# Two-layer mixer kernel: conditioning half moved, norm squares added on GpSimd, two scalars computed first

## The chip, the cores and the metric

One Trainium2 chip, and one of its cores. The number is the device time of one execution in microseconds (us); all arithmetic is fp32 or made of fp32 parts. TensorE is PE below, VectorE DVE, ScalarE ACT, GpSimd POOL and the engine that issues the weight transfers SP.

## The reference

Two blocks run one after the other. The first (`first_block`) works on 256 latent and 256 context tokens of width 1024 in two layers, and the change touches it alone, but for the norms, which the second block has too. Cut to what matters:

```python
def rms_norm(x, g, eps):
    return x * lax.rsqrt(jnp.mean(x * x, axis=-1, keepdims=True) + eps) * g

def mixer(h_lat, h_ctx, ...):
    lam = exp(sum(lv[0] * lv[1])) - exp(sum(lv[2] * lv[3])) + lam_init
    ...
    fa = fourier_mix(h_lat @ w_fa)
    db = diff_post(diff_attention_latent(qb, kb, vb, lam))      # softmax(s0) - lam * softmax(s1)
    nc = neighbourhood_attention_latent(...)
    g_a, g_b, g_c = split(sigmoid(h @ w_g + b_gate), 3)
    return (g_a * (fa @ w_a) + g_b * (db @ w_b) + g_c * (nc @ w_c)) @ w_out

for l in range(2):
    mod, mod_c = silu_c @ w_ada[l] + b_ada[l], silu_cc @ w_ada[l] + b_ada[l]
    sh1, sc1, gt1, sh2, sc2, gt2 = split(mod, 6)
    h = h + gt1 * mixer(modulate(rms_norm(h, g_mix[l]), sh1, sc1), ...)
    h = h + gt2 * conv_ffn(modulate(rms_norm(h, g_ffn[l]), sh2, sc2))
x = rms_norm(h, g_final)
```

The second block has stick-breaking attention, sparse attention and two more feed-forwards, with four norms of its own. `silu_c @ w_ada[l]` is the conditioning: one row of 1024 against 1024 x 6144 weights, for latent and context at once.

## The kernel before, in words

Activations lie feature-major in SBUF, 8 row-blocks of 128 features by T tokens: T is 512 in layer 0 and in the norm that ends it, 256 afterwards. Weights come from memory in slabs of 1 MB (SP, L951, a ring of three raw buffers). A slab is cut into pieces of 128 x 1024 numbers; there are four places for pieces. ACT copies a piece's high part (`split`, L1304), DVE takes the low part (L1585), and PE multiplies high by high, low by high and high by low (L1026 to L1028) for every 128 rows. The last piece of a slab frees the raw buffer.

The order of the work is written out by `Plan` as one list of steps, and the program of every engine walks that list. Nothing overtakes on an engine. `finish(gen)` writes out all steps of a generator; `weave(main, filler, n_main, n_fill)` writes units of attention and, after each, a share of filler steps; `mixed(a, b)` takes one step of each in turn. `later(n, f)` puts a step off by n ticks; attention units and filler steps tick. A `split` step is written whenever a place for a piece is free at the moment at which a gemm or the conditioning asks for its next piece (`ahead()`, called by `piece()`), and nowhere else.

**Conditioning** (`ada`): per four column blocks two slabs of two pieces each, PE with 8 matmuls of 4 x 256 high and 8 low per slab (L1057, L1058). The result's rows are copied by ACT (`ada_rows`, L1317) into a square buffer, turned on PE two ticks later (`ada_turn`, L1066), and added to the bias by DVE (L1602, L1604, L1609). Layer 1's 48 column blocks, 24 filler steps, run woven into the feed-forward (FFN) of layer 0.

**Neighbourhood attention** (`na1`, `na2`, `attend_pv`): 32 units (8 heads by 4 query blocks) in layer 0. Scores on PE (L1157), exp on ACT (L1460), then the probabilities are turned on PE (L1125), copied by ACT to a square buffer (`pT`, L1435), and multiplied with the values on PE (`pv`, L1142), one tick after the turn. Its filler is the second half of q and k and `merge(1, "w_b", ...)`: four quarters of two gate steps (sigmoid on ACT, L1358) and two product steps each. Differential attention is built the same way (scores L1118, exp L1429), and in layer 0 its filler already mixes conditioning steps of layer 0 with merge steps.

**Norm** (`NormPlan`): ACT squares each row-block (L1328), PE sums over the features with a matmul against ones (L1075, 8 of them into one bank; the trace shows each as two records), ACT takes the root (L1333), DVE the reciprocal (L1613) and the product (L1621), ACT scales, and the low parts are made by DVE (L1626) for even row-blocks and by POOL (L995) for odd ones. There are 11 norms. Two compute all squares at once (`mix0`, T=512, and one of T=256 between the second block's parts). Four hang on gemms of eight pieces deep, each square behind its row-block (`ffn0`, T=512, and three of T=256). Five hang on the last gemm of a feed-forward (one of T=512, `mix1`; four of T=256), whose last accumulation is two pieces deep and whose row-blocks therefore follow one another within a few us.

**lam**: after the split of `mix0` and of `mix1`, the product of 64 x 2 numbers on DVE (L1631), a sum on PE (L1081), exp on ACT and a subtraction on DVE.

Buffers: eight PSUM banks, four `tmps`, two square buffers (`sqs`), two gate buffers (`gts`). Each is given to the step that takes it next in turn, with a wait for its last reader.

Of the kernel before, what the change touches and what calls it, by code (L numbers as in the profile page):

```python
# [9 lines left out]
F32R = mybir.dt.float32r  # L10
# [4 lines left out]
NR = 3  # L15
# [130 lines left out]
class Plan:  # L146
# [276 lines left out]
    def layer(self, l, nrm):  # L423
# [7 lines left out]
        lb = self.banks.take()  # L431
        self.add("lam", (l,), b=lb)
        self.banks.give(lb, ("lam_exp", l))
# [113 lines left out]
        filler = itertools.chain(na_qk(1), merge(1, "w_b", 4, lambda k: ("db", l, k)))  # L547
        self.weave(self.run_units([(h, qt) for h in range(8) for qt in range(nq)], na1), filler, 8 * nq, 4 + 16)
# [3 lines left out]
        for k in range(8):  # L552
# [10 lines left out]
                   self.ada(1, 0, 48) if l == 0 else iter(()), 32, 24)  # L563
# [229 lines left out]
class NormPlan:  # L793
    def __init__(self, plan, name, T, at_once=None):
        self.plan, self.name, self.T, self.b, self.n, self.square = plan, name, T, None, 0, None
        if at_once:
            for k in range(8):
                self.add(k, at_once)

    def add(self, k, after):  # L800
        q = self.plan.sqs.take()
        self.plan.add("sq", (self.name,), n=k, t=q, x=(self.T, self.n == 0 and self.square is None, after))
        self.sum()
        self.square = (q, k)
# [153 lines left out]
def pool_program(pool, on, c, plan):  # L958
# [11 lines left out]
    for s in plan.steps:  # L970
# [14 lines left out]
        elif s.kind == "bias":  # L985
# [5 lines left out]
            load(("bias", l, h), BI[:, (h % 2) * 512:(h % 2) * 512 + 512], dram["nab"][l, h])  # L991
        elif s.kind == "nlow" and s.n % 2:
# [12 lines left out]
def tensor_program(pe, on, c, plan):  # L1005
# [5 lines left out]
    for s in plan.steps:  # L1011
# [56 lines left out]
        elif kind == "sqsum":  # L1068
            i, k = s.n
            if i == 0:  # L1070
                for f in s.b.was:
                    on.wait_ge(*at(*f))
            on.wait_ge(*at("side", "consts"))
            on.wait_ge(*at("sq", id[0], k))
            pe.matmul(c.bank(s.b)[:, 0:s.x], ones, c.sq(s.t)[:, 0:s.x], start=i == 0, stop=i == 7).then_inc(  # L1075
                up("acc", ("sqsum", id[0], i)), 1)
        elif kind == "lam":
            for f in s.b.was:
                on.wait_ge(*at(*f))
            on.wait_ge(*at("lam_pp", *id))  # L1080
            pe.matmul(c.bank(s.b)[:, 0:2], ones[0:64, :], c.m["ST"][0:64, 20:22], start=True, stop=True).then_inc(  # L1081
# [205 lines left out]
def scalar_program(act, on, c, plan, nc):  # L1287
# [6 lines left out]
    for s in plan.steps:  # L1294
# [23 lines left out]
        elif kind == "sq":  # L1318
            T, first, after = s.x
            if first:  # L1320
# [240 lines left out]
def vector_program(dve, on, c, plan):  # L1561
# [15 lines left out]
    for s in plan.steps:  # L1577
# [513 lines left out]
```

## Time and profile before

| | us |
|---|---|
| median of 3 runs | 3034.61 |
| lowest and highest | 3031.26, 3041.79 |
| the profiled execution's time | 3040.34 |
| its span in the profile | 3038.5 |
| PE busy, PE weight loads busy | 2787.8, 2422.3 |
| DVE, ACT, POOL busy | 1754.9, 1406.3, 57.2 |
| mean granted clock of PE | 0.949 |

A row of the timeline is the start in us, the duration in us, engine, line, operation, target and sources, size and count, and in brackets how long the engine had been idle and what released it. Matmuls of PE overlap: a duration holds the latency of one, and the distance of two starts is their pace. In the waits view a row is engine, tile and line of the waiter, the engine, tile and line that released it, then us in total, times and the longest.

### The profile page before, as it was taken

Reading aid. Unit: us, or ns where it says so; the run is one execution under the profiler, and the core shown is the slowest. Engines: PE = TensorE matmul, PEld = TensorE weight load, DVE = VectorE, ACT = ScalarE, POOL = GpSimd, SP = SyncE. Lnnn points to the kernel's source line nnn. Section 1 sums busy time; section 2 is a strip of 40 time slices with the busy share of each in tenths; the row PEclk is TensorE's granted clock in tenths of the full one; section 3 lists DMA queues with packets and bytes.
Section 4 is the critical chain, followed back from the end, with each engine's and each line's share of the span. In section 5 each row is a group of like instructions: output and inputs, shape, how many; then the busy total and the mean of one; then the engine's idle time right before and its main releaser. Section 6 shows DMA issues by size and latency. Waiting matters only on the chain.

```text
span 3038.5 us, 42732 instructions
## 1 busy us (share of the span) xinstructions
PE 2787.8 (92%) x17980; PEld 2422.3 (80%) x17980; DVE 1754.9 (58%) x2928; ACT 1406.3 (46%) x2258; POOL 57.2 (2%) x75
## 2 busy tenths in 40 slices
PE   4997899998999997989989979989998999789999
PEld 2875576676777775877789979987998999667999
DVE  5255634345666665454568756656566657565565
ACT  5245635433444444464655544445444545433443
POOL 1000000000000000000000000000000000000000
PEclk7998999999999998999999989999999999776999
DMA  6223422121444432223345545542455555200454
GB/s 224 66 90 111 145 76 67 53 95 64 153 139 136 142 132 97 91 98 104 112 141 192 167 144 183 175 130 83 154 183 164 169 194 167 86 28 1 153 181 139
DMA packets 337391, 382.16 MB, mean 126 GB/s; under 512 B 7408, under 2 KB 301296, under 8 KB 337200
## 3 DMA queue, kind: packets, MB, share of 16 engines
q1 hardware_dynamic: 334656, 370.37, 37.0%
q0 software_dynamic: 2544, 9.06, 0.9%
q8 instruction: 142, 2.33, 0.3%
q14 instruction: 49, 0.40, 0.0%
HBM read 378.36 MB, written 1.05 MB: 125 GB/s over the span
## 4 chain that ended last, share of the span: by engine, by line
PE 80%; DVE 10%; ACT 7%; issue 2%; DMA 1%; POOL 0%; DVEq 0%; ACTq 0%; POOLq 0%
PE PS L1026 21%; PE PS L1028 20%; PE PS L1027 20%; PE PS L1142 2%; ACT WH L1304 2%; DVE WL L1585 2%; DVE TMP L1621 2%; PE PS L1043 1%; PE PS L1044 1%; PE PS L1045 1%; PE PS L1075 1%; PE PS L1157 1%; PE PS L1282 1%; PE PS L1125 1%; DVE RS L1613 1%
## 5 line engine op out<-in xcount | busy, mean ns | idle before, releaser
L1585 DVE TENSOR_TENSOR WL<-RAWB,WH 128x1024 fp32r<-128x1024 f32 (+1 forms) x709 | 845.9, 1203 | 659.2 <-ACT WH L1304 658.1
L1026 PE MATMUL PS<-AH,WH 128*128 128x256 f32 (+1 forms) x3072 | 980.7, 319 | 55.3 <-DVE AL L1626 44.0
L1027 PE MATMUL PS<-AL,WH 128*128 128x256 f32 (+1 forms) x3072 | 963.7, 314 | 0.0
L1028 PE MATMUL PS<-AH,WL 128*128 128x256 f32 (+1 forms) x3072 | 963.1, 314 | 0.0
L1304 ACT ACTIVATE WH<-RAWB 128x1024 fp32r<-128x1024 f32 (+1 forms) x709 | 725.0, 1036 | 349.3 <-PE PS L1028 308.5
L1026 PEld LDWEIGHTS PS<-AH,WH 128*128 128x128 f32 x3072 | 589.6, 192 | 126.8 <-DVE AL L1626 45.5
L1028 PEld LDWEIGHTS PS<-AH,WL 128*128 128x128 f32 x3072 | 589.8, 192 | 34.8
L1027 PEld LDWEIGHTS PS<-AL,WH 128*128 128x128 f32 x3072 | 590.6, 192 | 32.2 <-issue 0.2
L1026 PE MATMUL PS<-BH,WH 128*128 128x256 f32 (+1 forms) x1504 | 480.7, 320 | 7.0 <-DVE BL L1722 3.0
L1027 PE MATMUL PS<-BL,WH 128*128 128x256 f32 (+1 forms) x1504 | 463.1, 308 | 0.0
L1028 PE MATMUL PS<-BH,WL 128*128 128x256 f32 (+1 forms) x1504 | 462.8, 308 | 0.0
L1026 PEld LDWEIGHTS PS<-BH,WH 128*128 128x128 f32 x1504 | 284.6, 189 | 39.4 <-issue 16.2
L1027 PEld LDWEIGHTS PS<-BL,WH 128*128 128x128 f32 x1504 | 284.8, 189 | 17.5 <-issue 3.1
L1028 PEld LDWEIGHTS PS<-BH,WL 128*128 128x128 f32 x1504 | 284.6, 189 | 15.1
L1389 ACT ACTIVATE F<-PS,PV 128x512 f32<-128x512 f32 (+1 forms) x88 | 58.8, 668 | 186.8 <-PE PS L1028 186.8
L1057 PE MATMUL PS<-WH,SC 128*4 128x256 f32 x384 | 96.6, 289 | 41.5 <-DVE WL L1585 41.4
L1758 DVE SCALAR_TENSOR_TENSOR F<-PS,PV,F 128x255 f32<-128x255 f32 x132 | 63.1, 478 | 98.0 <-ACT F L1389 97.4
L1043 PE MATMUL PS<-WH,AH 128*128 128x256 f32 x352 | 101.7, 289 | 0.0
L1044 PE MATMUL PS<-WL,AH 128*128 128x256 f32 x352 | 100.7, 286 | 0.0
L1751 DVE SCALAR_TENSOR_TENSOR H<-PS,MOD,H 128x256 f32<-128x256 f32 x168 | 73.5, 477 | 46.5 <-PE PS L1028 46.0
L1045 PE MATMUL PS<-WH,AL 128*128 128x256 f32 x352 | 100.1, 284 | 0.0
L1058 PE MATMUL PS<-WL,SC 128*4 128x256 f32 x384 | 95.8, 287 | 0.0
(259 smaller groups left out, 2824.7 us busy)
## 6 DMA issues: line engine op xcount, KB each, us to landing
RAWB<-in_f_in SPq DMA_DIRECT2D x88, 1024.0 KB, 5.0
RAWB<-in_w_in SPq DMA_DIRECT2D x52, 1024.0 KB, 4.9
RAWB<-in_w_ada SPq DMA_DIRECT2D x48, 1024.0 KB, 5.2
RAWB<-in_w_up SPq DMA_DIRECT2D x44, 1024.0 KB, 5.2
RAWB<-in_f_out SPq DMA_DIRECT2D x40, 1024.0 KB, 4.9
RAWB<-in_w_down SPq DMA_DIRECT2D x20, 1024.0 KB, 5.0
RAWB<-in_sb_qkv SPq DMA_DIRECT2D x12, 1024.0 KB, 4.9
RAWB<-in_w_out SPq DMA_DIRECT2D x8, 1024.0 KB, 5.1
```

The source lines that it names most:

```text
L1026: pe.matmul(out, h, xh[:, 0:T], start=k == 0, stop=False)
L1027: pe.matmul(out, h, xl[:, 0:T], start=False, stop=False)
L1028: i = pe.matmul(out, l, xh[:, 0:T], start=False, stop=k == g.kt - 1)
L1043: pe.matmul(out, h, wh, start=k == 0, stop=False)
L1044: pe.matmul(out, h, wl, start=False, stop=False)
L1045: i = pe.matmul(out, l, wh, start=False, stop=k == 7)
L1057: pe.matmul(out, sc_v[:, 4 * i + k, :], hi[:, k, :], start=i == 0 and k == 0, stop=False)
L1058: t = pe.matmul(out, sc_v[:, 4 * i + k, :], lo[:, k, :], start=False, stop=i == 1 and k == 3)
L1304: act.activation(c.part("WH", p), c.raw(p.slab)[:, k0:k1, c0:c1], ACT.Copy).then_inc(up("hi", ("hi", p.p)), 1)
L1585: dve.tensor_tensor(c.part("WL", p), c.raw(p.slab)[:, k0:k1, c0:c1], c.part("WH", p).bitcast(F32), ALU.subtract).then_inc(up("lo", ("lo", ...
L1751: t = stt(x, b[:, q * 256:q * 256 + 256], c.mod(l, part, n, q), x, ALU.mult, ALU.add)
L1758: stt(x[:, a + 1:e], b[:, a:e - 1], c.sm(f"conv_w{l}", n, 1), x[:, a + 1:e], ALU.mult, ALU.add).then_inc(up("vec", ("upb", g.name, n, q)), 1)
```

## The change

Three things. The conditioning's first 24 column blocks of layer 1 become filler of layer 0's neighbourhood attention, mixed step by step with its merge, and 24 blocks stay in the feed-forward. A norm's first square goes to a gate buffer, six are added to it by POOL one after another (`sqadd`), the eighth stays in its square buffer, and PE makes two sums instead of eight, both when `split` asks for them. The scalars `lam` of both layers are made at the start, before the first conditioning step. Parts that only give `lam` its own columns are left out here.

```diff
@@ -428,9 +428,6 @@
         w_in, a = ("w_in", l), f"mix{l}"
         ready = lambda k: ("xlo", a, k)
         nrm.split(a, T, [("G1", l, 0, (l, 0))] + [("G1", l, 1, (l, 0))], 512)
-        lb = self.banks.take()
-        self.add("lam", (l,), b=lb)
-        self.banks.give(lb, ("lam_exp", l))
...
             self.attend_pv("na", ("na", l, h, qt), p, n // 128, out_bank, then, 3 if l == 0 else 2)
-        filler = itertools.chain(na_qk(1), merge(1, "w_b", 4, lambda k: ("db", l, k)))
-        self.weave(self.run_units([(h, qt) for h in range(8) for qt in range(nq)], na1), filler, 8 * nq, 4 + 16)
+        ada = self.ada(1, 0, 24) if l == 0 else iter(())
+        filler = itertools.chain(na_qk(1), self.mixed(merge(1, "w_b", 4, lambda k: ("db", l, k)), ada))
+        self.weave(self.run_units([(h, qt) for h in range(8) for qt in range(nq)], na1), filler, 8 * nq,
+                   4 + 16 + (12 if l == 0 else 0))
         self.finish(merge(2, "w_c", 0, lambda k: ("nc", l, k)))
 
...
         self.wide = Ring(self, 12)
         nrm = NormPlan(self, f"mix{l + 1}" if l == 0 else "final", T)
         self.weave(self.ffn(f"c{l}", ("w_up", l), ("w_down", l), T, lambda k: ("xlo", b, k), "up_conv", "res", (l, 5), nrm),
-                   self.ada(1, 0, 48) if l == 0 else iter(()), 32, 24)
+                   self.ada(1, 24, 48) if l == 0 else iter(()), 32, 12)
         return nrm
...
         self.add("start")
+        for l in range(2):
+            lb = self.banks.take()
+            self.add("lam", (l,), b=lb)
+            self.banks.give(lb, ("lam_exp", l))
         self.finish(self.ada(0, 0, 16))
         nrm = self.layer(0, NormPlan(self, "mix0", 512, ("side", "ctxT")))
         nrm = self.layer(1, nrm)
...
+
+
     def __init__(self, plan, name, T, at_once=None):
-        self.plan, self.name, self.T, self.b, self.n, self.square = plan, name, T, None, 0, None
+        self.plan, self.name, self.T, self.n, self.acc, self.last = plan, name, T, 0, None, None
         if at_once:
             for k in range(8):
                 self.add(k, at_once)
 
     def add(self, k, after):
-        q = self.plan.sqs.take()
-        self.plan.add("sq", (self.name,), n=k, t=q, x=(self.T, self.n == 0 and self.square is None, after))
-        self.sum()
-        self.square = (q, k)
+        plan, i = self.plan, self.n
+        self.n += 1
+        if i == 0:
+            self.acc = plan.gts.take()
+        q = plan.sqs.take() if i else None
+        plan.add("sq", (self.name,), n=i, b=self.acc, t=q, p=k, x=(self.T, after))
+        if 0 < i < 7:
+            plan.add("sqadd", (self.name,), n=i, b=self.acc, t=q, x=self.T)
+            plan.sqs.give(q, ("sqadd", self.name, i))
+        elif i == 7:
+            self.last = q
 
     def sum(self):
-        if self.square is None:
+        if self.last is None:
             return
-        plan, (q, k) = self.plan, self.square
-        self.square = None
-        if self.b is None:
-            self.b = plan.banks.take()
-        i = self.n
-        self.n += 1
-        plan.add("sqsum", (self.name,), n=(i, k), b=self.b, t=q, x=self.T)
-        plan.sqs.give(q, ("sqsum", self.name, i))
-        if i == 7:
-            plan.add("rstd", (self.name,), b=self.b, n=self.T, x=plan.rs_was)
-            plan.banks.give(self.b, ("sd", self.name))
+        plan, q = self.plan, self.last
+        self.last = None
+        b = plan.banks.take()
+        plan.add("sqsum", (self.name,), b=b, t=(self.acc, q), x=self.T)
+        plan.sqs.give(q, ("sqsum", self.name))
+        plan.gts.give(self.acc, ("sqsum", self.name))
+        plan.add("rstd", (self.name,), b=b, n=self.T, x=plan.rs_was)
+        plan.banks.give(b, ("sd", self.name))
...
@@ -989,6 +998,12 @@
             else:
                 on.wait_ge(*at("na_add", l, h - 2, 1))
             load(("bias", l, h), BI[:, (h % 2) * 512:(h % 2) * 512 + 512], dram["nab"][l, h])
+        elif s.kind == "sqadd":
+            acc = c.gt(s.b)[:, 0:s.x]
+            on.wait_ge(*at("sq", s.id[0], s.n))
+            if s.n > 1:
+                on.wait_ge(*at("sqadd", s.id[0], s.n - 1))
+            pool.tensor_tensor(acc, acc, c.sq(s.t)[:, 0:s.x], ALU.add).then_inc(up("sums", ("sqadd", s.id[0], s.n)), 1)
...
         elif kind == "sqsum":
-            i, k = s.n
-            if i == 0:
-                for f in s.b.was:
-                    on.wait_ge(*at(*f))
+            for f in s.b.was:
+                on.wait_ge(*at(*f))
             on.wait_ge(*at("side", "consts"))
-            on.wait_ge(*at("sq", id[0], k))
-            pe.matmul(c.bank(s.b)[:, 0:s.x], ones, c.sq(s.t)[:, 0:s.x], start=i == 0, stop=i == 7).then_inc(
-                up("acc", ("sqsum", id[0], i)), 1)
+            on.wait_ge(*at("sqadd", id[0], 6))
+            pe.matmul(c.bank(s.b)[:, 0:s.x], ones, c.gt(s.t[0])[:, 0:s.x], start=True, stop=False)
+            on.wait_ge(*at("sq", id[0], 7))
+            pe.matmul(c.bank(s.b)[:, 0:s.x], ones, c.sq(s.t[1])[:, 0:s.x], start=False, stop=True).then_inc(
+                up("acc", ("sqsum", id[0])), 1)
...
         elif kind == "sq":
-            T, first, after = s.x
-            if first:
+            T, after = s.x
+            if s.n == 0:
                 on.wait_ge(*at("eps"))
                 act.activation(EPS[:, 2:3], EPS[:, 0:1], ACT.Sqrt)
                 if id[0] == "mix0":
                     on.wait_ge(*at("side", "xT"))
             on.wait_ge(*at(*after))
-            for f in s.t.was:
-                on.wait_ge(*at(*f))
-            act.activation(c.sq(s.t)[:, 0:T], H[:, s.n, 0:T], ACT.Square).then_inc(up("acted", ("sq", id[0], s.n)), 1)
+            for f in (s.t if s.n else s.b).was:
+                on.wait_ge(*at(*f))
+            act.activation((c.sq(s.t) if s.n else c.gt(s.b))[:, 0:T], H[:, s.p, 0:T], ACT.Square).then_inc(
+                up("acted", ("sq", id[0], s.n)), 1)
         elif kind == "rstd":
-            on.wait_ge(*at("sqsum", id[0], 7))
+            on.wait_ge(*at("sqsum", id[0]))
```

On PE, in layer 0's neighbourhood attention, where a merge step ends. L1026 to L1028 are the gemm's matmuls (now L1041 to L1043), L1125 the turn (now L1142), L1142 the product with the values (now L1159), L1157 the scores (now L1174); L1072 is the conditioning, before L1057. Before:

```order
L1026 MATMUL PS<-AH,WH 128x512
L1027 MATMUL PS<-AL,WH 128x512
L1028 MATMUL PS<-AH,WL 128x512
L1142 MATMUL PS<-SQ,F 64x128 x2
L1125 MATMUL PS<-CC,TMP 128x128 x4
L1157 MATMUL PS<-F 128x256
L1026 MATMUL PS<-AH,WH 128x512
```

and with the change:

```order
L1042 MATMUL PS<-AL,WH 128x512
L1043 MATMUL PS<-AH,WL 128x512
L1142 MATMUL PS<-CC,TMP 128x128 x4
L1159 MATMUL PS<-SQ,F 64x128 x4
L1174 MATMUL PS<-F 128x256
L1072 MATMUL PS<-WH,SC 4x256
L1073 MATMUL PS<-WL,SC 4x256
```

Before, a unit's turn stands behind another unit's product, and a filler step lies between it and its own product. Now a unit's turn stands directly before its own product.

On ACT, in the same stage, around a gate step. L1358 is the sigmoid (now L1376), L1435 the copy of a turned unit (now L1453), L1460 the exp (now L1478), L1304 the high part of a piece (now L1321), L1334 the copy of the conditioning's rows. Before:

```order
L1304 ACTIVATE WH<-RAWB 128x1024
L1358 ACT_TABLE_LOAD
L1358 ACTIVATE GT<-PS,PV 128x512
L1435 ACTIVATE SQ<-PS 128x512
L1460 ACT_TABLE_LOAD
L1460 ACTIVATE TMP,ST<-PS,ST 128x512
L1435 ACTIVATE SQ<-PS 128x256
L1460 ACTIVATE TMP,ST<-PS,ST 128x512
L1304 ACTIVATE WH<-RAWB 128x1024
```

and with the change:

```order
L1453 ACTIVATE SQ<-PS 128x512
L1376 ACT_TABLE_LOAD
L1376 ACTIVATE GT<-PS,PV 128x512
L1478 ACT_TABLE_LOAD
L1478 ACTIVATE TMP,ST<-PS,ST 128x256
L1321 ACTIVATE WH<-RAWB 128x1024 x4
L1453 ACTIVATE SQ<-PS 128x512
L1334 ACTIVATE SQ<-PS 4x512
L1478 ACTIVATE TMP,ST<-PS,ST 128x512
```

Before, one high part stands between two units. Now four stand in a row, behind an exp and its table load and ahead of the next unit's copy.

## Rows read from the trace of the kernel before

**Rows 1.** The profile's page, part 1: busy us, share of the span, instructions.

```profile
PE 2787.8 (92%) x17980; PEld 2422.3 (80%) x17980; DVE 1754.9 (58%) x2928; ACT 1406.3 (46%) x2258; POOL 57.2 (2%) x75
```

**Rows 2.** Timeline: row-blocks of a gemm without (79 to 85) and with a norm.

```profile
79.19 0.60 ACT L1365 ACTIVATE F<-PS 128x512 f32<-128x512 f32 x1 [5.69 <-PE PS L1028]
84.79 0.60 ACT L1365 ACTIVATE F<-PS 128x512 f32<-128x512 f32 x1 [4.06 <-PE PS L1028]
...
702.89 0.59 PE L1075 MATMUL PS<-SQ,CC 128*128 128x512 f32 x1
...
709.32 0.59 PE L1075 MATMUL PS<-SQ,CC 128*128 128x512 f32 x1
```

**Rows 3.** Timeline: end of a feed-forward, T=256, two pairs of row-blocks.

```profile
1979.04 0.75 ACT L1328 ACTIVATE SQ<-H 128x256 f32<-128x256 f32 x2 [1.63 <-DVE H L1773]
1979.50 0.70 PE L1075 MATMUL PS<-SQ,CC 128*128 128x256 f32 x2 [0.76 <-ACT SQ L1328]
1979.69 1.04 ACT L1304 ACTIVATE WH<-RAWB 128x1024 fp32r<-128x1024 f32 x1
...
1982.83 1.13 PE L1075 MATMUL PS<-SQ,CC 128*128 128x256 f32 x4 [0.77 <-ACT SQ L1328]
```

**Rows 4.** The source view of L995: ns min/median/max, first and last start, forms.

```profile
L995 POOL TENSOR_TENSOR AL<-TMP,AH x44: 726/792/1501, 63.0 to 2846.3; 128x256 fp32r<-128x256 f32 x32, 128x512 fp32r<-128x512 f32 x12
```

**Rows 5.** Timeline: `mix0`, first squares and the root.

```profile
44.20 1.13 ACT L1328 ACTIVATE SQ<-H 128x512 f32<-128x512 f32 x2
...
53.95 0.69 ACT L1333 ACTIVATE RS<-PS,EPS 128x512 f32<-128x512 f32 x1 [1.22 <-PE PS L1075]
```

**Rows 6.** Timeline: root and first copy-out after it, `ffn0` and `mix1`.

```profile
718.71 0.69 ACT L1333 ACTIVATE RS<-PS,EPS 128x512 f32<-128x512 f32 x1 [1.22 <-PE PS L1075]
...
739.22 0.78 ACT L1389 ACTIVATE F<-PS,PV 128x512 f32<-128x512 f32 x1 [2.40 <-PE PS L1028]
...
1172.71 0.69 ACT L1333 ACTIVATE RS<-PS,EPS 128x512 f32<-128x512 f32 x1 [1.22 <-PE PS L1075]
...
1195.52 0.38 ACT L1365 ACTIVATE F<-PS 128x256 f32<-128x256 f32 x1 [3.26 <-PE PS L1028]
```

**Rows 7.** Timeline: ACT at the start of the program.

```profile
17.22 1.06 ACT L1304 ACTIVATE WH<-RAWB 128x1024 fp32r<-128x1024 f32 x1 [6.96 <-DMA RAWB<-in_w_ada]
```

**Rows 8.** Waits of PE, neighbourhood attention of layer 0 (440 to 600).

```profile
PE PS L1142 <- ACT SQ L1435: 5.1, 7, 1.3
```

**Rows 9.** Timeline: differential attention of layer 0, a gate step, then conditioning.

```profile
349.48 0.63 PE L1125 MATMUL PS<-CC,TMP 128*128 128x128 f32 x4
...
350.87 1.28 ACT L1429 ACT_TABLE_LOAD   x1
...
352.17 0.47 ACT L1429 ACTIVATE TMP<-PS,ST 128x256 f32<-128x256 f32 x1
...
353.08 3.89 ACT L1304 ACTIVATE WH<-RAWB 128x1024 fp32r<-128x1024 f32 x4
...
355.44 0.38 PE L1057 MATMUL PS<-WH,SC 128*4 128x256 f32 x1 [3.69 <-DVE WL L1585]
```

**Rows 10.** Timeline: the same stage, conditioning behind a score of 512.

```profile
323.98 1.13 PE L1118 MATMUL PS<-F 64*128 64x512 f32 x4 [0.69 <-ACT F L1439]
...
329.57 0.28 PE L1057 MATMUL PS<-WH,SC 128*4 128x256 f32 x1 [3.44 <-DVE WL L1585]
```

**Rows 11.** Waits of PE, differential attention of layer 0 (160 to 380).

```profile
PE PS L1057 <- DVE WL L1585: 22.6, 8, 6.6
PE PS L1118 <- ACT SQ L1317: 7.1, 1, 7.1
```

**Rows 12.** Windows: stretch, us, busy PE, PEld, DVE, ACT, POOL, PE clock, DMA.

```profile
350.00:360.00 10.00, 6.31 (x36) 4.62 (x35) 6.47 (x10) 7.52 (x12) 0.00 (x0) 0.83 0.36 110
```

**Rows 13.** Waits of PE, feed-forward of layer 0 (745 to 1160).

```profile
PE PS L1026 <- DVE WL L1585: 6.2, 8, 1.0
PE PS L1066 <- ACT SQ L1317: 3.3, 3, 1.1
```

More of the change, by code:

```diff
@@ L1079, in tensor_program @@
                 on.wait_ge(*at(*f))
+            at_ = 20 + 4 * id[0]
+            on.wait_ge(*at("side", "consts"))
             on.wait_ge(*at("lam_pp", *id))
-            pe.matmul(c.bank(s.b)[:, 0:2], ones[0:64, :], c.m["ST"][0:64, 20:22], start=True, stop=True).then_inc(
+            pe.matmul(c.bank(s.b)[:, 0:2], ones[0:64, :], c.m["ST"][0:64, at_:at_ + 2], start=True, stop=True).then_inc(
                 up("acc", ("lam_sum",) + id), 1)
@@ L1348, in scalar_program @@
             on.wait_ge(*at("lam_sum", *id))
-            act.activation(ST[:, 22:24], c.bank(s.b)[:, 0:2], ACT.Exp).then_inc(up("acted", ("lam_exp",) + id), 1)
+            act.activation(ST[:, 22 + 4 * id[0]:24 + 4 * id[0]], c.bank(s.b)[:, 0:2], ACT.Exp).then_inc(up("acted", ("lam_exp",) + id), 1)
         elif kind == "ev":
@@ L1630, in vector_program @@
             lv = c.sm(f"lam{l}")[0:64, :].rearrange("p (a b) -> p a b", b=2)
-            dve.tensor_tensor(ST[0:64, 20:22], lv[:, :, 0], lv[:, :, 1], ALU.mult).then_inc(up("vec", ("lam_pp", l)), 1)
+            a = 20 + 4 * l
+            on.wait_ge(*at("side", "small"))
+            dve.tensor_tensor(ST[0:64, a:a + 2], lv[:, :, 0], lv[:, :, 1], ALU.mult).then_inc(up("vec", ("lam_pp", l)), 1)
             on.wait_ge(*at("lam_exp", l))
-            dve.tensor_scalar(LM[:, 0:1], ST[:, 23:24], ST[:, 22:23], -(0.8 - 0.6 * math.exp(-0.3 * l)), ALU.subtract,
+            dve.tensor_scalar(LM[:, 4 + l:5 + l], ST[:, a + 3:a + 4], ST[:, a + 2:a + 3], -(0.8 - 0.6 * math.exp(-0.3 * l)), ALU.subtract,
                               ALU.add).then_inc(up("vec", ("lam", l)), 1)
@@ L1673, in vector_program @@
             on.wait_ge(*at("da_rec", *id))
-            dve.tensor_tensor(ST[:, 8 + col:9 + col], ST[:, 11 + col:12 + col], LM[:, 0:1], ALU.mult).then_inc(
+            dve.tensor_tensor(ST[:, 8 + col:9 + col], ST[:, 11 + col:12 + col], LM[:, 4 + id[0]:5 + id[0]], ALU.mult).then_inc(
                 up("vec", ("da_lam",) + id), 1)
@@ L1943, in build @@
                    G1=sb("G1", [128, 2, 8, 2]), G2=sb("G2", [128, 2, 8, 2]), ST=sb("ST", [128, 32]),
-                   LM=sb("LM", [128, 4]), SC=sb("SC", [128, 32], F32R), EPS=sb("EPS", [128, 4]), RAWB=sb("RAWB", [128, NR, SLAB]),
+                   LM=sb("LM", [128, 8]), SC=sb("SC", [128, 32], F32R), EPS=sb("EPS", [128, 4]), RAWB=sb("RAWB", [128, NR, SLAB]),
                    WH=sb("WH", [128, NW, PIECE], F32R), WL=sb("WL", [128, NW, PIECE], F32R))
         mem["banks"] = [ctx.enter_context(nc.psum_tensor(f"PS{i}", [128, 512], F32)) for i in range(8)]
-        mem["sem"] = {n: sem(n) for n in ("acc", "hi", "acted", "lo", "vec", "xlo_pool")}
+        mem["sem"] = {n: sem(n) for n in ("acc", "hi", "acted", "lo", "vec", "xlo_pool", "sums")}
         mem["rawsem"] = [sem(f"raw{i}") for i in range(NR)]
```

## The prediction

> **What bounds the kernel.** I read part 1 of the page first: PE is busy 92% of the span, ACT and DVE about half, POOL hardly at all [rows 1]. So a part that takes work off PE gains what PE spent on it, a part that shortens a stretch in which PE stands still gains that stretch, and work moved between ACT, DVE and POOL counts only where PE waits for it. Then the timelines of the norms, to see what a sum costs; the waits of PE in the three stages between which the conditioning moves; and one timeline of the stage that already mixes conditioning with merge steps, as a template for what the attention will look like.
>
> A measurement of this kernel resolves about 0.3%, 9 us, between no change and a change.
>
> **Norms on gemms eight deep.** A row-block of 512 columns lasts 84.79 - 79.19 = 5.60 us without a sum and 709.32 - 702.89 = 6.43 with one [rows 2]: a sum costs PE .83 us, at 256 columns half, .42. Six of eight vanish; the squares and the adds lie beside 5.6 us (or 2.8) of matmuls, so all but the last are hidden. One norm of 512: 6 x .83 = -5.0. Three of 256: 3 x 6 x .42 = -7.6. Together **-12.6**.
>
> **Norms on the end of a feed-forward.** Two row-blocks take 1982.83 - 1979.50 = 3.33 us, with .83 for two sums and a PE wait of .76 for the squares [rows 3]. Afterwards ACT sets the pace: two squares .75 and a high part 1.04, some 1.9 a pair. At the end, the sixth add can start only behind the seventh square, and the two sums stand behind it. An add of 256 is priced by POOL's low-part subtraction, two fp32 inputs of the same size: .73 to .91, and 1.27 to 1.50 at 512; the row that groups them has .726, .792 and 1.501 as shortest, median and longest [rows 4]. So the end comes about 1 us later and the pairs gain 4.5: -3.5 in each of four, -4.3 at 512 columns: **-18.3**. Bounds: the whole of the six sums and their waits, -4.8 each (-24), and nothing where the chain of adds is late.
> The adds have DVE's two-input instructions beside them. [...]
>
> **Norms with all squares at once.** In `mix0` two squares of 512 end at 45.33 and the root comes at 53.95 [rows 5]; in between PE sums as fast as ACT squares. Now the chain is six adds of 1.27 to 1.50 plus .1 handover from 45.33: it ends near 54.5, then two sums, by then at half the clock since PE stood idle (2 x 1.7), root at 58: +4 (bounds +1.5 if the adds take 1.27 and the clock holds, +5). The one of 256 in the second block: six adds against eight sums of .42, behind two transfers that POOL issues: +2. Together **+6.0**.
>
> **lam.** From the root to the first copy-out, `ffn0` without lam takes 739.22 - 718.71 = 20.51 us, `mix0` 79.19 - 53.95 = 25.24, `mix1` 1195.52 - 1172.71 = 22.81 [rows 2, 5, 6]. All three split eight blocks of 512 columns; taking the rest for lam, -4.7 and -2.3, **-7.0**. At the start, two round trips PE, ACT, DVE with a table load of 1.28 stand before the first high part, some 3 us. They are covered by the transfers: ACT stood 6.96 us until 17.22 for a raw slab [rows 7], so only a remainder, **+0.5** (without that cover, +3).
>
> **Conditioning in the neighbourhood attention.** What leaves the feed-forward: waits of 6.2 and 3.3 us [rows 13], half of them, **-4.8**. The matmuls themselves only move. What comes in the attention has three parts.
> First, **turn before product**. PE waits 5.1 us in seven places there, mean .73 [rows 8]; those are the places where a unit's turn stands directly ahead of its own product, with ACT's copy between. With the change's order there are 26 (counted in the list of steps; one is shown). 26 x .73 = 19.0, less 5.1: **+13.9**. Lower bound: nothing, if ACT's copy is free of other work; the copy alone (.59) and the handover say half.
> Second, **bursts of high parts**. With a ring of four places and `ahead()` called only when a piece is asked for, a gate or product step holds the places, and the conditioning step after it writes four high parts at once, behind an exp. ACT needs 3.89 for four, and PE's second conditioning piece waits for the low part of the second one, 3.69 us in one template and 3.44 in the other [rows 9, 10]. The stage that mixes them today pays 22.6 us in eight such waits [rows 11]. Each of the three merge quarters mixed with conditioning gives two. Burst 1, behind a gate step: the template runs 355.44 - 349.48 = 5.96 from turn to matmul; add the sigmoid's table load, now behind the copy (1.28), add the turn for which that copy waits (.6), take off one exp of 256 (.46): 7.4. PE's own work in it: turn .63, its wait .75 (priced above), and product, score and one piece, taken as 2.4, a little over the 2.15 of a score of 512 and one piece in the template (329.57 - 323.98 - 3.44 [rows 10]): 3.8. Wait 3.6. Burst 2, behind a product step: 3.44 less one score and exp of 256, 2.9. 3 x 3.6 + 3 x 2.9 = **+19.5**. Bounds: 0 (DVE and ACT ahead) and 6 x 6.6, the longest.
> Third, **the clock**. The template's stretch 350 to 360 was granted .83 [rows 12], a loss of 1.7 us in 10. Two of the six in that way, **+3**. The load of an exp here starts at 350.87, and the exp at 352.17, 1.30 later: nothing but the load.
> The DMA issues move along with their steps. A wait stands on SP only for a piece's last low part, as today, and POOL's bias transfers in this stage have no adds ahead of them, since the stage has no norm.
>
> **Sum:** -12.6 - 18.3 + 6.0 - 7.0 + .5 - 4.8 + 13.9 + 19.5 + 3 = **+0.2**. Against the profiled execution's 3040.34 that is 3040.5; the median of the three runs is 5.7 lower, so I forecast 3034.61 + .2 = **3034.8 us**, no change that can be measured.
>
> **Rivals.**
> *A, faster, .34.* The attention has four times as many units as there are burst places, and ACT was busy less than half of the time: it may be ahead when a burst comes. Halve the bursts' waits (-9.8), let the clock stay up (-3), and the turn's wait be .55 instead of .73 (26 x .18 = -4.7): 3034.8 - 17.5 = **3017**. For it: only seven waits in the stage now, all short [rows 8]. Against it: the template pays [rows 11].
> *B, slower, .12.* After each burst the next score takes the bank that `ada_rows` (L1317) has just read. Behind four high parts and a copy, that ACT step ends after the product; from that point on PE's score waits as well. One place did so in the template, 7.1 us [rows 11]. At 3.5 more for six bursts, +21: **3056**. It decides when ACT, at the time of PE's product, still has two high parts ahead of the rows.
> *C, slower, .12.* The chain of adds is serial, and it is the only thing in the change that puts POOL on a path. If a link at 256 columns takes 1.7 us, the longest row of POOL [rows 4] and a handover of .2, six take 10.2 instead of the 6.6 in the sum: +3.6 in four ends, and .5 more for each of six adds in two norms of 512, +3 each: +20.4, **3055**. Against it: 32 of the 44 rows are of that smaller form, and the median is .79.
> *D, up to 3042.5, .04.* The start of the exp behind its table load speaks for a plain 1.28 [rows 9]. If two switches in a burst each cost as much again as the load itself, three bursts would cost 3 x 2 x 1.28 = 7.7 more, **3042.5**, still within what can't be told from nothing. [...]
> That the change does not do what it says can be left out: the lists of steps show two sums instead of eight, and the conditioning in the attention.
>
> **Chances.** My forecast .38, A .34, B .12, C .12, D .04. Faster by over .3%: A, **.34**. Within: forecast and D, **.42**. Slower: B and C, **.24**. The forecast's own spread is about 9 us on either side (the two largest terms, 18.3 and 19.5, each good to a third). The range reaches from a little below A to just short of the slower two: **3013 to 3054**.
>
> **What would show it.** In the waits of PE between 440 and 620: product behind the copy of the turned unit 26 times, near 19 us; conditioning behind DVE's low part 6 times, near 19.5. PE's busy time falls by the 66 sums, 35 us (18 of .83, 48 of .42). The pair of row-blocks at a feed-forward's end below 2.2 us. `mix0`'s root near 58, its first copy-out still earlier than 25.24 us behind it. Root to copy-out of `mix1` near 20.5. The forecast is wrong if the attention's conditioning waits come to under 8 us (then A) or if scores wait for `ada_rows` (then B), or if an add of 256 takes over 1.2 us (then C).

## The result, and the profile after

| | us |
|---|---|
| before, median of 4 | 3038.2 (3031.3 to 3046.4) |
| with the change, median of 4 | 3082.1 (3073.0 to 3090.5) |
| ratio | 1.0157, 95% interval 1.0126 to 1.0188 |
| the changed kernel's profiled execution: time, span | 3089.0, 3087.2 |
| its mean granted clock | 0.933 |

The change costs 44 us by the medians and 48 by the ratio, and the forecast had 0. Part 1 of the changed kernel's page, beside [rows 1]:

```profile
PE 2776.1 (90%) x17848; PEld 2414.9 (78%) x17848; DVE 1758.6 (57%) x2928; ACT 1410.7 (46%) x2259; POOL 115.7 (4%) x141
```

132 records of PE are gone (66 sums), but PE was busy for only 12 us less: matmuls ran longer. Cut at the 11 roots and at the first and last square before each, the two traces differ by 48.7 us, in these places:

| term | forecast | measured |
|---|---|---|
| four norms on gemms eight deep | -12.6 | -8.7 |
| five ends of a feed-forward | -18.3 | +11.5 |
| two norms at once | +6.0 | +5.4 |
| lam, and the start | -6.5 | -7.0 |
| attention and feed-forward of layer 0: waits | +28.6 | +26.1 |
| the same: the rest, the clock | +3 | +20.5 |
| all else | 0 | +0.9 |

The waits of the fifth row are -4.8 in the feed-forward, 19.1 - 5.1 for the turned copies and 16.9 in the bursts. The last row is not quiet: in it +10.3 us, spread over code that did not change, stand against -9.5 in one stretch near the end, of which the last section tells.

**The attention.** The waits of PE in the changed kernel between 430 and 660, to hold against [rows 8]:

```profile
PE PS L1072 <- DVE WL L1603: 16.9, 6, 3.3
PE PS L1159 <- ACT SQ L1453: 16.8, 22, 1.5
PE PS L1174 <- DVE BL L1737: 4.2, 3, 1.4
```

Six bursts and the turned copies, as forecast (19.5 in 6, 19.0 in 26; four more turned copies wait between 660 and 680, which makes 19.1 in 26). One burst in the timeline:

```profile
476.53 0.70 PE L1174 MATMUL PS<-F 64*128 64x256 f32 x2
...
477.48 1.28 ACT L1478 ACT_TABLE_LOAD   x1
...
478.77 0.47 ACT L1478 ACTIVATE TMP<-PS,ST 128x256 f32<-128x256 f32 x1
...
479.24 2.94 ACT L1321 ACTIVATE WH<-RAWB 128x1024 fp32r<-128x1024 f32 x3
480.32 2.36 DVE L1603 TENSOR_TENSOR WL<-RAWB,WH 128x1024 fp32r<-128x1024 f32 x2 [2.63 <-ACT WH L1321]
...
481.59 0.37 PE L1072 MATMUL PS<-WH,SC 128*4 128x256 f32 x1 [3.35 <-DVE WL L1603]
481.77 0.41 PE L1073 MATMUL PS<-WL,SC 128*4 128x256 f32 x1
```

The wait is 3.35, as in [rows 9, 10], and the matmuls behind it take .41 where they took .28 before it: the clock granted from 481 on was .50. The windows (columns as in [rows 12]) say how long that lasts. The kernel before, the changed one, and four stretches of the latter:

```profile
440.00:660.00 220.00, 213.45 (x972) 154.83 (x970) 90.40 (x160) 93.27 (x152) 2.68 (x5) 1.00 0.22 71
```

```profile
440.00:660.00 220.00, 180.58 (x844) 123.21 (x842) 93.34 (x169) 98.15 (x155) 2.69 (x5) 0.88 0.28 92
...
481.00:494.00 13.00, 11.72 (x34) 7.79 (x35) 6.73 (x9) 4.91 (x8) 0.00 (x0) 0.50 0.72 242
495.00:511.00 16.00, 11.34 (x64) 7.34 (x64) 8.00 (x18) 5.30 (x13) 0.54 (x1) 1.00 0.07 17
512.00:514.00 2.00, 2.00 (x10) 1.36 (x8) 2.00 (x3) 0.93 (x1) 0.00 (x0) 0.50 0.65 204
515.00:542.00 27.00, 22.40 (x116) 15.57 (x114) 7.90 (x18) 13.82 (x22) 0.54 (x1) 1.00 0.24 78
```

Each of the six bursts does that, and they come in two kinds, in turn. The three with a wait of 3.34 or 3.35 us (until 481.59, 543.01 and 604.72) leave some 13.7 us at half clock each; the three with 2.29 to 2.31 (until 511.40, 573.10 and 634.43) leave 3.4. That is 51 us at half clock, and PE was busy in 44 of them, so an estimate of what the slower pace cost is 44 / 2 = 22 us. Before, the same stretch of 220 us was granted 1.00 throughout.

**The end of a feed-forward**, T=256, against [rows 3]:

```profile
2028.12 0.75 ACT L1345 ACTIVATE SQ<-H 128x256 f32<-128x256 f32 x2 [1.63 <-DVE H L1793]
...
2028.62 1.59 POOL L1006 TENSOR_TENSOR GT<-GT,SQ 128x256 f32<-128x256 f32 x2 [2.26 <-ACT SQ L1345]
2028.78 1.04 ACT L1321 ACTIVATE WH<-RAWB 128x1024 fp32r<-128x1024 f32 x1
2029.85 1.44 DVE L1603 TENSOR_TENSOR WL<-RAWB,WH 128x1024 fp32r<-128x1024 f32 x1 [1.43 <-ACT WH L1321]
2031.22 0.74 DVE L1793 SCALAR_TENSOR_TENSOR H<-PS,H 128x256 f32<-128x256 f32 x2
...
2031.66 0.75 ACT L1345 ACTIVATE SQ<-H 128x256 f32<-128x256 f32 x2 [1.84 <-DVE H L1793]
...
2035.20 0.75 ACT L1345 ACTIVATE SQ<-H 128x256 f32<-128x256 f32 x2 [1.84 <-DVE H L1793]
2035.70 0.72 POOL L1006 TENSOR_TENSOR GT<-GT,SQ 128x256 f32<-128x256 f32 x1 [1.95 <-ACT SQ L1345]
2036.57 1.19 PE L1088 MATMUL PS<-GT,CC 128*128 128x256 f32 x2 [8.13 <-POOL GT L1006]
2037.55 1.06 PE L1090 MATMUL PS<-SQ,CC 128*128 128x256 f32 x2
2038.65 0.47 ACT L1351 ACTIVATE RS<-PS,EPS 128x256 f32<-128x256 f32 x1 [2.70 <-PE PS L1090]
```

Follow the rows round: two squares, a high part, its low part on DVE, two copies to H on DVE, two squares again. That loop is the pair's time, 2031.66 - 2028.12 = 3.54 us against 3.33 before. Six of PE's eight sums are gone and the pair is no shorter, so the sums were not what set it. It grew by .21, which is the low part's 1.44 against 1.22 beside POOL's add. At the end ACT stands 2.70 us before the root, and before the change it was .89:

```profile
1984.00 0.47 ACT L1333 ACTIVATE RS<-PS,EPS 128x256 f32<-128x256 f32 x1 [0.89 <-PE PS L1075]
```

Most of the loss lies there: from the last square to the root the five ends take 10.6 us more, and from the first square to the last .9. With 512 columns the low part is held up longer:

```profile
1201.05 2.74 POOL L1006 TENSOR_TENSOR GT<-GT,SQ 128x512 f32<-128x512 f32 x2 [2.62 <-ACT SQ L1345]
...
1202.74 2.13 DVE L1603 TENSOR_TENSOR WL<-RAWB,WH 128x1024 fp32r<-128x1024 f32 x1 [1.65 <-ACT WH L1321]
```

**Norms at once and lam**: the root of `mix0`, its first copy-out, then those of `mix1`, against [rows 5, 6]:

```profile
57.57 0.69 ACT L1351 ACTIVATE RS<-PS,EPS 128x512 f32<-128x512 f32 x1 [4.62 <-PE PS L1090]
...
78.09 0.60 ACT L1383 ACTIVATE F<-PS 128x512 f32<-128x512 f32 x1 [2.40 <-PE PS L1043]
...
1216.88 0.69 ACT L1351 ACTIVATE RS<-PS,EPS 128x512 f32<-128x512 f32 x1 [4.49 <-PE PS L1090]
...
1237.42 0.38 ACT L1383 ACTIVATE F<-PS 128x256 f32<-128x256 f32 x1 [2.44 <-PE PS L1043]
```

20.52 and 20.54 us between them, where there were 25.24 and 22.81.

### The profile page after: what moved, and what is told of

Read it like the earlier page. It is cut to its first block, busy times and chain, and to the rows that moved or that the text cites. A ratio compares the mean times of both kernels' runs of the same rounds, so it can differ in the third digit from the quotient of the medians.

```text
span 3087.2 us, 42579 instructions
## 1 busy us (share of the span) xinstructions
PE 2776.1 (90%) x17848; PEld 2414.9 (78%) x17848; DVE 1758.6 (57%) x2928; ACT 1410.7 (46%) x2259; POOL 115.7 (4%) x141
## 3 DMA queue, kind: packets, MB, share of 16 engines
q8 instruction: 141, 2.31, 0.3%
HBM read 378.36 MB, written 1.05 MB: 123 GB/s over the span
## 4 chain that ended last, share of the span: by engine, by line
PE 77%; DVE 11%; ACT 9%; issue 2%; DMA 1%; POOL 1%; POOLq 0%; ACTq 0%; DVEq 0%
PE PS L1041 20%; PE PS L1043 20%; PE PS L1042 20%; DVE WL L1603 3%; ACT WH L1321 3%; PE PS L1159 2%; DVE TMP L1639 2%; PE PS L1058 1%; PE PS L1060 1%; PE PS L1059 1%; PE PS L1174 1%; PE PS L1299 1%; PE PS L1142 1%; ACT SQ L1453 1%; DVE RS L1631 1%
## 5 line engine op out<-in xcount | busy, mean ns | idle before, releaser
L1041 PE MATMUL PS<-AH,WH 128*128 128x256 f32 (+1 forms) x3072 | 985.0, 321 | 75.9 <-DVE AL L1644 61.5
L1043 PE MATMUL PS<-AH,WL 128*128 128x256 f32 (+1 forms) x3072 | 966.8, 315 | 0.0
L1321 ACT ACTIVATE WH<-RAWB 128x1024 fp32r<-128x1024 f32 (+1 forms) x709 | 725.7, 1037 | 347.9 <-PE PS L1043 307.1
L1041 PEld LDWEIGHTS PS<-AH,WH 128*128 128x128 f32 x3072 | 592.3, 193 | 156.0 <-DVE AL L1644 54.7
L1043 PEld LDWEIGHTS PS<-AH,WL 128*128 128x128 f32 x3072 | 592.8, 193 | 34.8
L1041 PE MATMUL PS<-BH,WH 128*128 128x256 f32 (+1 forms) x1504 | 470.1, 313 | 8.3 <-DVE BL L1742 3.0
L1043 PE MATMUL PS<-BH,WL 128*128 128x256 f32 (+1 forms) x1504 | 465.5, 310 | 0.0
L1041 PEld LDWEIGHTS PS<-BH,WH 128*128 128x128 f32 x1504 | 286.0, 190 | 40.7 <-issue 16.2
L1043 PEld LDWEIGHTS PS<-BH,WL 128*128 128x128 f32 x1504 | 285.9, 190 | 15.7
L1072 PE MATMUL PS<-WH,SC 128*4 128x256 f32 x384 | 100.6, 296 | 49.4 <-DVE WL L1603 49.3
L1006 POOL TENSOR_TENSOR GT<-GT,SQ 128x256 f32<-128x256 f32 (+1 forms) x66 | 58.4, 884 | 1866.2 <-ACT SQ L1345 1863.3
L1159 PE MATMUL PS<-SQ,F 128*64 128x128 f32 (+1 forms) x480 | 74.1, 297 | 35.3 <-ACT SQ L1453 34.3
```

Source lines behind the costliest of these rows:

```text
L1041: pe.matmul(out, h, xh[:, 0:T], start=k == 0, stop=False)
L1043: i = pe.matmul(out, l, xh[:, 0:T], start=False, stop=k == g.kt - 1)
L1072: pe.matmul(out, sc_v[:, 4 * i + k, :], hi[:, k, :], start=i == 0 and k == 0, stop=False)
L1159: t = pe.matmul(out, v[j], c.sq(s.t)[:, j * 128:j * 128 + 128], start=j == 0, stop=j == nk - 1)
L1321: act.activation(c.part("WH", p), c.raw(p.slab)[:, k0:k1, c0:c1], ACT.Copy).then_inc(up("hi", ("hi", p.p)), 1)
```

## The experiments

Ratios are to the kernel before, run on the same chip beside them (medians 3038.7 to 3041.4).

**1. One part alone.** `ada_only` has the two hunks of the diff in `layer`, `sq_only` those of `NormPlan` and its steps, `lam_only` those of lam, `no_ada` all but the first.

> Only the conditioning is moved. Theory P (parts add up, read from the two traces): +46.6 us in layer 0 between the root of mix0 and the first square of mix1, nothing elsewhere: +40 to +50 against the kernel before. Waits of the conditioning for DVE's low part near 17 us in 6 places, of the product for the turned copy near 17, and a granted clock below 0.9 in the attention. Rival Q: the waits are caused together with the changed norms or scalars (shifted rings); then well under +30 here.

> Only the norms' squares are added on GpSimd. Theory P: gemm norms -8.6 us, ends of feed-forwards +11.5, norms at once +5.4: +8. Root of mix0 3.4 later behind its last square, and DVE's low part 1.44 us beside a GpSimd add of 256 columns, about 2.1 beside one of 512, against 1.22. Rival R (my forecast): the ends gain too once the attention is undisturbed: -20 or better.

> Only the scalars are made at the start. Theory P: -4.7 us in mix0 and -2.3 in mix1, nothing at the start (the first square of mix0 still at 44.2): -7 in the profile, within what the rounds can just tell. Rival: the start is delayed by the two round trips, then -4 or less.

> The changed kernel with the conditioning back in the feed-forward. Theory P: +8.3 - 7.0 = +1 against the kernel before, no change. Rival Q (parts act on one another): clearly slower, +10 or more.

Measured: `ada_only` 1.0150 (1.0123 to 1.0176), +46 us. `sq_only` 0.9994 (0.9980 to 1.0007). `lam_only` 0.9985 (0.9969 to 1.0001). `no_ada` 0.9979 (0.9960 to 0.9999), -6. The whole loss is the moved conditioning, alone and undisturbed by the rest; its trace has 19.1 us in 26 waits for the turned copy, the 26 x .73 of the forecast, and 17.0 in 6 for the low part. `lam_only` brings its -4.7 and -2.3 between root and copy-out again. The squares as a whole are worth nothing that can be measured. By place `sq_only` has -8.4 in the gemms, +11.4 in the ends and +5.4 at once, a sum of +8.4, as expected; its time came out 10 better than that sum, and so neither +8 nor the -20 of rival R was met. `no_ada` is 7 better than its expected +1 as well. What may stand behind that is in the last section.

**2. Bursts, turns and the clock.** The list of steps shows where a burst comes from. A gate gemm's two steps use two pieces, and a product gemm's two steps one. With conditioning between those two steps, later pieces are used first; the place that comes next in the ring is the one still held, so no high part is written, and when it is released four are. `na_pairs` takes both steps of merge before a step of conditioning, `na_t2` puts the turn off by two ticks, `na_pairs_t2` does both (all on `ada_only`):

```diff
-            for g in list(gens):
+            for i in turns:
+                g = (a, b)[i]
...
-            self.attend_pv("na", ("na", l, h, qt), p, n // 128, out_bank, then, 3 if l == 0 else 2)
+            self.attend_pv("na", ("na", l, h, qt), p, n // 128, out_bank, then, 2 if l == 0 else 2)
...
+        filler = itertools.chain(na_qk(1), self.mixed(merge(1, "w_b", 4, lambda k: ("db", l, k)), ada, (0, 0, 1)))
```

> The conditioning moved alone (ada_only), and the turn of a unit in layer 0's neighbourhood attention put off by two ticks instead of three: 2 instead of 26 units have their turn directly ahead of their own product; the six bursts of four high parts stay. Theory B (bursts hold the clock down, turn waits cost their own length only): waits for the turned copy from 19.1 us to under 3, the clock in the attention still under 0.92, time +46 becomes about +30. Theory S (short waits in their number hold the clock down as well): clock near 1, +46 becomes +15 or less.

> The conditioning moved alone, but mixed as two merge steps, then one of conditioning, so that pieces are used in the order of their numbers: the list of steps has no burst of four high parts any more, 15 of two; the 26 turns ahead of their own product stay. Theory B: the conditioning's waits for DVE's low part fall from 17.0 us to under 3, the clock in the attention stays at 1.0, and +46 becomes +14 to +20 (19.1 of turn waits less 5.1, less what the feed-forward gains). Theory S: the clock stays low, +30.

> Both: pairs of merge steps and a turn after two ticks. If the two waits and the clock are all there is to the loss, nothing of the +46 is left and the feed-forward's gain stands: -3 to -10 against the kernel before. Rival: ACT itself is short in the attention (more high parts there), +5 or more stays with other names.

Measured: `na_t2` 1.0104 (1.0066 to 1.0142), +32; `na_pairs` 1.0111 (1.0070 to 1.0152), +34; both 0.9994 (0.9969 to 1.0019), -2. The two edits alone take off 14 and 12, together 47. Between 440 and 660 the granted clock is .88 in `ada_only`, .91 in `na_t2`, .90 in `na_pairs` and .96 with both. In `na_t2` theory B holds: .9 us in two waits for the turned copy, 16.2 in six for the low part. In `na_pairs` it missed, for it expected a clock of 1.00 and +14 to +20. Waits of PE, 430 to 680, in `na_pairs`:

```profile
PE PS L1147 <- ACT SQ L1440: 31.4, 30, 3.5
PE PS L1162 <- DVE BL L1722: 1.4, 1, 1.4
```

and in `na_pairs_t2`:

```profile
PE PS L1130 <- DVE BL L1722: 3.5, 1, 3.5
PE PS L1147 <- ACT SQ L1440: 2.3, 2, 1.8
PE PS L1062 <- DVE WL L1590: 1.8, 1, 1.8
```

With pairs alone the low-part waits are gone, but the turned copy, with two high parts ahead of it on ACT, is later: 12 us of the 17 only change their name. Six of the 30 waits last 2.07 to 3.47 us, and the clock falls behind five of these, and also behind one of 1.7 and one of 1.1. With both, the waits are nearly as short as before the move (8.2 us in all, against 6.5) and nothing of the loss is left.

`na_warm` is `ada_only` with its waits filled; PE makes this before each late piece, into a bank of its own that nobody reads:

```diff
+            for i in range(10):
+                t = pe.matmul(c.bank(s.b)[:, 0:128], ones, ones, start=i == 0, stop=i == 9)
```

> The conditioning moved alone (ada_only), with ten matmuls of ones by ones, 128 columns, .21 us each, that nobody reads, put on PE directly before each of the six conditioning pieces whose low part is late. Theory K (the standstill lowers the clock, and the slower clock costs on top of the wait): the waits for the low part fall from 17.0 us to about 5 since the time is filled, the wall time of those places is the same, the clock between 440 and 660 goes from .88 to .95 or better, and 8 to 15 us of the +46 go. Rival W (all of the loss is waiting; a lower clock only makes PE arrive later where it would wait anyway): +46 stays within 4 us.

Measured: 1.0074 (1.0053 to 1.0094), +22 instead of +46. Its timeline and its window:

```profile
478.67 2.39 PE L1078 MATMUL PS<-CC 128*128 128x128 f32 x20
...
482.17 0.28 PE L1063 MATMUL PS<-WH,SC 128*4 128x256 f32 x1 [1.11 <-DVE WL L1597]
...
440.00:660.00 220.00, 194.00 (x1062) 141.06 (x1061) 100.50 (x181) 105.02 (x166) 2.68 (x5) 1.00 0.30 99
```

The pieces come no earlier, the clock never falls, and half of the loss goes. So theory K holds, with more than the 8 to 15 us that it expected: of 46 us about 24 were the clock (good to some 10 by the intervals of the two ratios) and 22 standstill. The estimate from the windows above was 22. The 21.8 us of turned-copy waits that stay, .5 to 1.5 each, do not lower it: from 440 to 660 it is 1.00, against .88 in `ada_only`.

**3. The order at a feed-forward's end.** `tail_order` changes the kernel before, `tail_order_sq` is the same edit on `sq_only`:

```diff
-                    self.evac(g, c * 4 + j, b, hook)
+                    self.evac(g, c * 4 + j, b)
+                    if hook and j % 2:
+                        self.ahead()
+                        for n in (c * 4 + j - 1, c * 4 + j):
+                            hook.add(n, ("ev", g.name, n))
```

> The kernel before, with one thing changed: in the last gemm of each feed-forward the two squares of a pair of row-blocks are written behind the next high part, and the low part behind both copies to H. Theory L (the pair's 3.33 us are a loop over ACT's squares and high part, DVE's low part and copy; PE's sums are not in it): the pair goes to 2.2 to 2.8 us, each of five ends is 2 to 4 us shorter, -10 to -18 in all. Theory PE (my forecast's: PE's sums and ACT's busy time set the pace): the pair stays within 0.2 of 3.33, no change.

> The squares added on GpSimd (as in sq_only), and the two squares of a pair of row-blocks at a feed-forward's end written behind the next high part (as in tail_order). In tail_order the loop went over PE, whose sum waited for squares that waited for a high part that waited for PE. Here PE has no sum until the end. Theory L2 (what sets the pace is always a loop between engines in the order of the steps, not the busiest engine): with the loop cut, a pair of 256 columns takes 2.1 to 2.6 us instead of 3.54, the four ends are 2 to 3 us shorter each than in sq_only, -10 to -15 against sq_only in all ends. Theory C (GpSimd's chain, two adds of 1.6 a pair, and DVE beside it set it): the pair stays over 3.2, nothing gained.

Measured: `tail_order` 1.0038 (1.0016 to 1.0061), slower. Both theories missed. Its timeline:

```profile
1991.82 0.81 PE L1079 MATMUL PS<-SQ,CC 128*128 128x256 f32 x2
1992.06 1.06 ACT L1308 ACTIVATE WH<-RAWB 128x1024 fp32r<-128x1024 f32 x1 [3.56 <-PE PS L1032]
...
1993.02 0.70 ACT L1332 ACTIVATE SQ<-H 128x256 f32<-128x256 f32 x2
...
1993.47 0.70 PE L1079 MATMUL PS<-SQ,CC 128*128 128x256 f32 x2 [0.84 <-ACT SQ L1332]
```

The high part now waits for the pair's matmuls to release its place, the squares stand behind it, and PE's next sum waits for them. I had cut one loop and closed a wider one, through PE: 3.6 us from one high part to the next where the granted clock was .97 (1992.06 to 1995.63), 5.2 where it was .50 (1986.82 to 1992.06).
`tail_order_sq` 0.9992 (0.9972 to 1.0012), no change. ACT and POOL at one end:

```profile
1975.10 0.40 ACT L1344 ACTIVATE GT<-H 128x256 f32<-128x256 f32 x1
...
1976.66 0.71 ACT L1344 ACTIVATE SQ<-H 128x256 f32<-128x256 f32 x2
...
1981.75 0.88 ACT L1344 ACTIVATE SQ<-H 128x256 f32<-128x256 f32 x2
```

```profile
1977.13 6.65 POOL L1007 TENSOR_TENSOR GT<-GT,SQ 128x256 f32<-128x256 f32 x5 [0.52 <-ACT SQ L1344]
```

Four pairs of squares begin within 6.65 us, 2.2 a pair, as L2 said. But five adds last the same 6.65, the squares between wait for a buffer that an add has to release, and the root comes 3.38 behind the end of the last square. By the trace the five ends are 8 us better than in `sq_only`, short of L2's 10 to 15, and no better than on PE: once the loop is cut, the chain of adds sets it. That is part of theory C, and of rival C.

**4. Where the squares pay, and the same disorder elsewhere.** `gemm_pool` keeps the adds for `ffn0`, `ffn1`, `ffn2_norm0` and `ffn2_norm1` and gives the other norms their old sums. `da_pairs` is the kernel before with `mixed` in turns of two and two in the differential attention.

> Squares added on GpSimd only in the four norms on gemms eight deep; the ends of the feed-forwards and the norms at once sum on PE as before. If the trace's split of sq_only by place holds: -8.6 us (-5.1, -0.1, -1.6, -1.6), nothing elsewhere.

> The kernel before, with one thing changed: in layer 0's differential attention conditioning and merge are mixed two and two instead of one and one, so that pieces are used in the order of their numbers. Theory O (bursts of four high parts come from a place that an unfinished pair of steps holds, whatever the stage): the list has one burst of four instead of eight, the waits of 22.6 us for the low part fall under 8, and the stage is 15 to 30 us shorter, the clock's share with it. Rival T: as in na_pairs the wait only changes its name, to the turned copies: within 5 us of no change.

Measured: `gemm_pool` 0.9948 (0.9929 to 0.9968), -16 us, with -5.1, -0.1, -1.6 and -1.6 at the four places: again some 7 better than its places. `da_pairs` 0.9919 (0.9897 to 0.9941), -25 us. Its waits in that stage, against [rows 11]:

```profile
PE PS L1145 <- ACT SQ L1438: 7.3, 4, 4.2
PE PS L1128 <- DVE TMP L1683: 6.3, 3, 3.4
PE PS L1060 <- DVE WL L1588: 3.1, 3, 1.4
```

Theory O holds: 22.6 became 3.1, and the one wait of 7.1 for the conditioning's rows is gone. Some of it shows under other names: the first two rows have 13.6, where the copies had 5.0 before. The granted clock of the stage (160 to 380) went from .92 to .95.

**5. Put together.** `best_a`: lam, squares everywhere but at once, `tail_order`, `da_pairs`. `best_b`: lam, `gemm_pool`, `da_pairs`. `best_c`: `best_b` with the conditioning moved as in `na_pairs_t2`.

> Scalars at the start, squares on GpSimd but for the two norms at once, squares at the ends behind the high part, and the differential attention mixed two and two; the conditioning stays in the feed-forward. By the parts: -7 (scalars) -8.6 (gemm norms) -10 (ends, if theory L2 holds; +11 if not) and whatever da_pairs gives.

> Scalars at the start, squares on GpSimd in the four norms on gemms eight deep only, differential attention mixed two and two; ends of the feed-forwards and norms at once as before, conditioning in the feed-forward. By the parts: -7 -8.6 -21 = -37 against the kernel before, and 5 better than best_a by the ends' five differences in the traces (+.2, +3.3, +.3, +1.3, -.2), less than the rounds can tell.

> best_b with half of layer 1's conditioning in the neighbourhood attention, mixed after every pair of merge steps, turn after two ticks. Theory P (parts add up; na_pairs_t2 was within 2 of before): within 5 us of best_b. Rival: the attention's remaining waits are worth more once the rest is shorter, +10.

Measured: 0.9853 (0.9830 to 0.9876), 0.9847 (0.9826 to 0.9868) at 2993.7 us, and 0.9855 (0.9827 to 0.9882). All three are 44 to 47 us faster than the kernel before, 7 to 10 more than the 37 that the parts of `best_b` gave, and cannot be told apart. `best_b` is the simplest, and the conditioning in the attention brings it nothing.

## Why the prediction was wrong

The forecast of no change was a balance: +31.6 us for the conditioning against -24.9 for the squares and -6.5 for lam. Two steps failed. The larger is the ends of the feed-forwards, 29.8 us between forecast and trace; the other is the price of the clock, 17.5. With the ends at their +11.5 the sum alone would have given some 3065, slower; with the clock at +20.5 alone, 3052.

- **Turn before product, right.** 26 x .73 = 19.0; 19.1 in 26 waits in `ada_only`.
- **Bursts, right.** +19.5 forecast, 16.9 in six.
- **What leaves the feed-forward, right.** Its two waits went from 9.5 to 4.7 us, -4.8.
- **Ends of a feed-forward, the step whose mechanism was wrong.** "Afterwards ACT sets the pace: two squares .75 and a high part 1.04, some 1.9 a pair." What sets it is the loop ACT, DVE, ACT, and I had summed busy times of engines instead of following what each square waits for. The rows for it were there [rows 3]: the squares waited 1.63 for DVE's H, and PE's sums .76 for the squares. So the 4.5 us a norm that the pairs were to gain did not come (+.9 in all five), and the end, taken as 1 us later, came 1.8 to 1.9 later at 256 columns and 3.3 at 512. -18.3 became +11.5.
- **The clock, the step whose size was wrong.** "Two of the six in that way, +3" took one window of a stage that is disturbed by itself anyway, and left four bursts at nothing. In a stage that stood at 1.00 each of the six lowered the clock; `na_warm` puts that at 24 us. The mechanism was named and its size was off eightfold. The traces of the stage agree: three times 13.7 and three times 3.4 us at half clock, 22 us lost by the estimate above.
- **Contention of DVE and POOL.** I noted that the adds have DVE's two-input instructions beside them, and put nothing into the sum for what they cost DVE. The add's price was right (.72 to 1.30), the neighbour's was not: 1.22 became 1.38 to 1.47 in 14 low parts, and 2.08 and 2.13 in two. Over these 16 it is 5.0 us of DVE's time.
- **Sums on gemms.** .83 at 512 columns, right (5.1 in six). "At 256 columns half, .42" was wrong: 1.55 in six, .26 each, in two of the three norms, and .6 in six in the third, where the first four row-blocks took 3.05 us with and without a sum. The timeline of the end had it, a sum at 1980.75 and the next matmul at 1981.00.
- **At once and lam, right**: root of `mix0` at 57.57 for 58, its two sums at a granted .52 (53.75 to 57.57) after PE had stood 10.5 us; 20.52 and 20.54 us to the copy-out; no delay at the start.
- **Rivals.** None was it. B and C had the right sign by other mechanisms. No score waited for the conditioning's rows, and an add of 256 took .72 to .75 (one of 48 took .97), so C's 1.7 a link was wrong, though the late root is its chain. The range ended 28 us below the result: no case let the ends and the clock fail together.

## What to carry to other kernels

Where filler shares a ring of buffers with the work it fills, let it come in whole units of that ring: interleaving inside a unit holds a place out of order, and the copies then come in bursts. Where a stage was granted the full clock, a standstill of PE like these six can cost more than its length again: 17 us of waits came with some 24 of clock, by far the most of it behind the three longer ones. Matmuls that nobody needs, put into the gap, show the clock's share (.88 to 1.00 here, and +46 us to +22). Price a stretch whose engines are all half idle by the loop that its waits form, not by its busiest engine. Count what an add on GpSimd costs DVE too: a low part of 1.22 us took .16 to .91 longer beside one here, 5.0 us over 16.

## What the runs showed of the hardware

DVE's low part of 1024 columns took 1.22 us (the median of its line, before and after). Where it overlapped an add of POOL by .36 us (2029.85 to 2030.21) it took .22 longer, and by 1.05 (1202.74 to 1203.79) .91 longer. In all 16 cases of the changed kernel's trace the add ran already when the low part began, and the low part ended 1.08 to 1.09 us behind the add's end, whatever the overlap: of its own 1.22 us all but .14 lay behind the add's end. Once a short low part of .56 us began first (2658.92); it kept its .56, and the add that began inside it took .97 instead of .73.

The clock differs between traces in one stretch of unchanged code, the sparse attention near the end. Here it is from the root of the last norm but one to the first square of the last, in the kernel before and in `lam_only`, where it begins within .2 us of the same time:

```profile
2603.55:2813.16 209.61, 180.04 (x878) 142.01 (x879) 122.21 (x394) 84.29 (x279) 3.09 (x4) 0.69 0.07 25
```

```profile
2603.42:2797.85 194.43, 163.18 (x878) 130.63 (x879) 121.27 (x394) 83.49 (x279) 3.08 (x4) 0.76 0.08 27
```

Both have the same 878 records of PE, and the second is 15 us shorter at a clock of .76 instead of .69. In the profiles of `lam_only`, `sq_only`, `no_ada`, `gemm_pool` and the best versions that stretch is 15 to 18 us shorter, in the changed kernel's 9.5 and in `ada_only`'s 6.8; in `da_pairs`, `na_t2`, `na_pairs`, `na_pairs_t2` and `na_warm` it is not. That is a good part of the spread of a kernel's own runs (3020 to 3047 before), and it may be why the totals of `sq_only`, `no_ada`, `gemm_pool` and the best versions are better than their places. Each kernel has one profile, so that is not shown, and what decides it stays open.
